# A two-block transformer kernel: the mixer's input products taken from x before its norm, the norm's row factor applied when the products leave PSUM, and retention's value products placed beside attention

## The chip, the core and the metric

One core of one Trainium2 chip runs the whole program. The metric is the device time of one execution in microseconds (us). The engines are PE (TensorE, matmuls into PSUM; its weight loads are listed as PEld), DVE (VectorE), ACT (ScalarE), POOL (GpSimd) and SP, whose queue issues all DMAs. Each engine works through its own list of instructions in order and waits on semaphores that the others raise.

## The reference, cut to what matters

Only the first steps of the first block are touched. x is 512 x 1024, float32, and everything is computed in float32.

```python
def rms_norm(x, g):
    y = x * lax.rsqrt(jnp.mean(x * x, axis=-1, keepdims=True) + RMS_EPS)
    return y * g

def hybrid_mixer(h, w_in, attn_gn_g, ret_gn_g, w_out):      # h = rms_norm(x, pre_mix_g)
    proj = h @ w_in                                        # 1024 -> 7 x 512
    aq, ak, av, rq, rk, rv, rg = jnp.split(proj, splits, axis=-1)
    a = dilated_attention(rope(aq), rope(ak), av)          # 8 heads of 64
    a = a * lax.rsqrt(jnp.mean(a * a, axis=-1, keepdims=True) + RMS_EPS)
    r = retention(rope(rq), rope(rk), rv)                  # 4 heads of 128
    r = silu(rg) * group_norm(r)
    return concat(a, r) @ w_out
```

Behind it come a cross-attention to a memory (`mem`, 256 rows, which has its own norm and value and key products), a SwiGLU, and a second block. They stay as they are.

## The kernel before

**Tiling.** x lies transposed in SBUF: 8 tiles of 128 features x 512 tokens (`XT`). A float32 product is made as three matmuls of rounded operands (`three`, L376): each operand is split into a high part (rounded to float32r) and a low part (the rest), and high x low, low x high and high x high are summed in PSUM. A 128 x 1024 chunk of weights (512 KB) is loaded into one of six slots, its high part is made by ACT (`hi_to`, L349; two buffers, so chunk i waits until chunk i-2 has been used), its low part by DVE (`lo_to`, L359). One chunk feeds 24 matmuls of 128x512 (three per k tile). Chunks are used in the order aq (0 to 3), ak (4 to 7), av (8 to 11), rq, rk, rg (12 to 23), rv (24 to 27), then the memory's values (28 to 35).

**Start of the mixer** (`mix_in_*`, L498 to L563). SP loads the 8 tiles of x, the tables `c0`, the gains (`small`), six weight chunks and the table `c1`. ACT squares the tiles of x, PE sums them over the features with a matrix of ones (`sums_pe`, 8 float32 matmuls, two buffers for the squares, so ACT and PE take turns), ACT makes the root (`root_act`: Ln and Exp), DVE multiplies each tile by gain and row factor (`scaled_dve`), ACT rounds the high part (`high_act`) and DVE takes the low part. Only then can the first product start. Then come the 8 tiles of q and k (`QK`), one weight chunk each: 24 matmuls, ACT's eviction from PSUM to SBUF, one float32 matmul with a permutation (`permA`) that turns the just evicted tile for the rotary embedding, and DVE's three operations of `rotate_dve`. PE waits in every tile for the eviction. Last come the 96 matmuls of av.

**Rest and attention** (`mix_rest_*`, `attend_*`). Python generators are interleaved by `weave` (L189): in each slot one step of the products of rq, rk and rg, one step of attention, and one more step of products. Attention has 32 units (4 query blocks x 8 heads) in 40 slots (`attend_slots`, L646): in slot n the scores of unit n, the transposition of unit n-2 and the value product of unit n-3; after the last unit of a query block its output is divided, squared on POOL, normed, multiplied on POOL (`a_gn`) and transposed by PE. The products of the rest are used up after 22 slots.

**Retention and memory** (`mid_*`). The order of each engine is written out as a string of letters (`TURNS0`, L795; `walk_streams`): r is the products of rv (PE) or their evictions (ACT), m the memory's norm, s retention's scores (DVE: the decay that takes them out of PSUM), i its outputs, w the rounding of the next weight chunk, V the memory's value products, M on ACT a Silu of a small vector, t a transposition. PE's scores and the row sum take four PSUM banks in turn (`low`). The memory's norm begins with 15 operations of 128x256 on POOL (`mem_pool`), which start when `mem` has been loaded; SP issues that load only when all events of the list `mixed` have come.

## Time and profile before

| | us |
|---|---|
| median of 3 runs | 2443.28 (2442.37 to 2444.06) |
| the profiled execution | 2444.46 |
| its span in the trace | 2442.6 |
| PE busy / DVE / ACT / POOL | 2338.0 / 1291.4 / 961.9 / 343.1 |
| mean granted PE clock | 0.985 |

The stages that the change touches lie in the first 306 us of the span: the start of the mixer until 114.6, rest and attention until about 249, the products of rv until about 274, retention until 294, then the memory's values. The profiled execution took 1.2 us more than the median. A granted clock of 1.00 is 2.4 GHz and 0.50 is 1.2 GHz. A float32 matmul shows as two records, a matmul of rounded operands as one.

### The profile page before, as it was taken

How to read it: one execution, taken by the hardware profiler on the slowest of the kernel's cores; microseconds unless marked ns; L12 is line 12 of the kernel's file. 1: busy time of each engine (PE TensorE's matmuls, PEld its weight loads, DVE VectorE, ACT ScalarE, POOL GpSimd, SP SyncE). 2: the span in 40 equal slices, each digit the busy share in tenths (PEclk: the TensorE clock that was granted, in tenths of full speed). 3: DMA queues.
4: the chain of work that ended last, by engine and by line, in shares of the span. 5: the costliest groups of instructions: out<-in, count | busy, mean ns of one | idle time of the engine just before them, and what ended most of it. 6: DMA issues, size and time to landing. Idle time of an engine off the chain costs nothing.

```text
span 2442.6 us, 29369 instructions
## 1 busy us (share of the span) xinstructions
PE 2338.0 (96%) x11798; PEld 1880.8 (77%) x11798; DVE 1291.4 (53%) x1982; ACT 961.9 (39%) x1672; POOL 343.1 (14%) x338
## 2 busy tenths in 40 slices
PE   6999998989999997999999999999999999899999
PEld 3677787768878884899998898776666788688887
DVE  3344547457757426766666777424464533542442
ACT  3235344443222225544534545345544422431331
POOL 0000214131101110232222333100111001000000
PEclk9999998999999998999999999999999999899999
DMA  4220222225565222110000011110101334232332
GB/s 159 78 67 29 83 99 96 86 104 172 185 212 188 62 74 80 61 57 27 27 27 18 18 35 53 35 53 20 41 20 53 104 109 135 70 97 95 95 98 83
DMA packets 60037, 195.69 MB, mean 80 GB/s; under 512 B 6656, under 2 KB 11520, under 8 KB 59520
## 3 DMA queue, kind: packets, MB, share of 16 engines
q1 hardware_dynamic: 59904, 193.83, 24.1%
q8 instruction: 94, 1.54, 0.3%
q14 instruction: 39, 0.32, 0.0%
HBM read 187.25 MB, written 6.55 MB: 79 GB/s over the span
## 4 chain that ended last, share of the span: by engine, by line
PE 89%; DVE 7%; ACT 2%; issue 1%; POOL 1%; DMA 0%; SPq 0%; DVEq 0%; ACTq 0%
PE ps L132 84%; PE ps L135 4%; DVE sb L165 2%; DVE sb L157 2%; DVE r L157 1%; ACT sb L144 1%; ACT r L144 1%; DVE r L165 1%; POOL sb L157 0%; ACT L142 0%; DVE sb L162 0%; DMA sb<-in_w_aq 0%; POOL sb L148 0%; SPq L186 0%; POOL sb L162 0%
## 5 line engine op out<-in xcount | busy, mean ns | idle before, releaser
L132 PE MATMUL ps<-r 128*128 128x512 f32 (+1 forms) x7032 | 1606.1, 387 | 46.4 <-DVE r L157 20.3
L132 PEld LDWEIGHTS ps<-r 128*128 128x128 f32 x7032 | 1282.7, 190 | 328.2 <-issue 48.1
L132 PE MATMUL ps<-sb 128*128 128x128 f32 (+5 forms) x3768 | 694.8, 332 | 49.4 <-ACT sb L144 32.0
L157 DVE TENSOR_TENSOR r<-sb,r 128x1024 fp32r<-128x1024 f32 (+3 forms) x413 | 431.1, 1054 | 446.4 <-ACT r L144 445.4
L132 PEld LDWEIGHTS ps<-sb 128*128 128x128 f32 x3768 | 505.2, 191 | 196.3 <-issue 110.1
L144 ACT ACTIVATE r<-sb 128x1024 fp32r<-128x1024 f32 (+3 forms) x437 | 377.9, 884 | 601.3 <-PE ps L132 452.1
L157 POOL TENSOR_TENSOR sb<-sb 128x512 f32<-128x512 f32 (+3 forms) x222 | 265.6, 1203 | 1552.4 <-ACT sb L144 990.8
L144 ACT ACTIVATE sb<-ps 128x512 f32<-128x512 f32 (+2 forms) x526 | 232.5, 462 | 515.8 <-PE ps L132 340.7
L157 DVE TENSOR_TENSOR sb<-ps,sb 128x512 f32<-128x512 f32 (+3 forms) x274 | 162.2, 602 | 214.0 <-PE ps L132 207.1
L165 DVE SCALAR_TENSOR_TENSOR sb<-sb 128x512 f32<-128x512 f32 (+5 forms) x232 | 242.8, 1057 | 38.4 <-ACT sb L144 36.3
L144 ACT ACTIVATE sb<-sb 128x512 f32<-128x512 f32 (+6 forms) x300 | 153.8, 528 | 75.2 <-POOL sb L157 26.2
L157 DVE TENSOR_TENSOR sb<-sb 128x512 f32<-128x512 f32 (+2 forms) x158 | 129.4, 819 | 92.7 <-ACT sb L144 88.2
L135 PE MATMUL ps<-sb 128*128 128x128 f32 (+1 forms) x998 | 144.4, 275 | 5.6 <-POOL sb L157 4.6
L165 DVE SCALAR_TENSOR_TENSOR sb<-ps,sb 128x128 f32<-128x128 f32 (+1 forms) x232 | 86.7, 412 | 117.7 <-PE ps L132 111.7
L135 PEld LDWEIGHTS ps<-sb 128*128 128x128 f32 (+1 forms) x998 | 115.2, 142 | 33.7 <-issue 12.0
L144 ACT ACTIVATE sb<-ps,sb 128x128 f32<-128x128 f32 (+3 forms) x181 | 82.2, 465 | 126.6 <-PE ps L132 126.0
L142 ACT ACT_TABLE_LOAD x67 | 86.0, 1283 | 71.5 <-PE ps L132 46.0
L162 DVE TENSOR_SCALAR sb<-sb 128x1 f32<-128x1 f32 (+6 forms) x136 | 65.1, 484 | 49.2 <-ACT sb L144 46.2
L157 DVE TENSOR_TENSOR sb<-sb,ps 128x512 f32<-128x512 f32 (+2 forms) x128 | 60.7, 484 | 46.5 <-PE ps L132 45.7
L162 POOL TENSOR_SCALAR sb<-sb 128x128 f32<-128x128 f32 x80 | 56.7, 715 | 175.4 <-PE ps L132 125.3
L148 DVE COPY sb<-ps 128x512 f32<-128x512 f32 (+5 forms) x76 | 38.4, 512 | 38.8 <-PE ps L135 31.8
L145 ACT ACTIVATE sb<-ps,sb 128x768 f32<-128x768 f32 (+1 forms) x48 | 39.1, 819 | 25.3 <-DVE sb L162 19.5
(24 smaller groups left out, 189.3 us busy)
## 6 DMA issues: line engine op xcount, KB each, us to landing
sb<-in_w_mlp SPq DMA_DIRECT2D x64, 512.0 KB, 3.5
sb<-in_w_mod SPq DMA_DIRECT2D x48, 512.0 KB, 4.6
sb<-in_w_qkv SPq DMA_DIRECT2D x24, 512.0 KB, 3.7
sb<-in_w_g SPq DMA_DIRECT2D x20, 512.0 KB, 3.9
sb<-in_w_u SPq DMA_DIRECT2D x20, 512.0 KB, 4.0
sb<-in_w_out SPq DMA_DIRECT2D x16, 512.0 KB, 3.6
sb<-in_w_down SPq DMA_DIRECT2D x16, 512.0 KB, 3.7
sb<-in_w_gate SPq DMA_DIRECT2D x16, 512.0 KB, 3.7
```

The source lines that it names most:

```text
L132: return QUIET if self.e is None else self.e.matmul(o, l, r, start=start, stop=stop)
L135: return QUIET if self.e is None else self.e.transpose(o, i, ident)
L142: self.e.preload_act_table_set(self.set)
L144: return self.e.activation(o, i, f, bias=bias, scale=scale)
L145: return self.e.activation(o, i, f, bias=bias, scale=scale, accum_out=acc)
L148: return QUIET if self.e is None else self.e.tensor_copy(o, i)
L157: return QUIET if self.e is None else self.e.tensor_tensor(o, a, b, op)
L162: return self.e.tensor_scalar(o, a, s1, None, op0) if op1 is None else self.e.tensor_scalar(o, a, s1, s2, op0, op1)
L165: return QUIET if self.e is None else self.e.scalar_tensor_tensor(o, a, s, b, op0, op1)
```

## The change

1. **Start.** The gains are loaded first, then two tiles of x and one weight chunk in turn. ACT rounds x times gain (without the row factor) as each tile arrives, DVE takes the low part from it. The products of aq start from that: `w_aq` is now stored by rows, and `project_four` makes all four tiles of q at once in four banks, chunk by chunk. Squares are made by ACT beside it and added up on POOL (`add_squares`); PE sums them in two matmuls (`row_sum_pe`) after aq. The row factor lies in `RX` (along tokens) and, by four transpositions, in `RCOL` (one per partition).
2. **Row factor at eviction.** q, k, rq, rk are evicted by DVE with a multiplication by `RX`, rg too, before ACT's Silu; av and rv by ACT with the scale `RCOL`. ACT evicts no q, k, rq or rk tile any more.
3. **Turnings later.** The matmul with `permA` runs at least one tile after its product (`swap`); three of them lie between the chunks of av. The table `c1` is loaded in two parts.
4. **rv beside attention.** After 16 empty steps the 96 matmuls of rv follow in `mix_rest_pe`, in slots 30 to 37 of attention; their weight chunks are rounded there. The order strings lose PE's r and move w, s and m; SP waits for the last score (`a_s`, 31) instead of `mixed` before it loads `mem`. ACT and DVE wait for `mixed` in their own lists.

```diff
-C1 = {"maskA": 512, "cosA": 512, "sinA": 512, "cosR": 512, "sinR": 512, "decay": 2048, "permA": 128, "permR": 128}
+C1 = {"permA": 128, "cosA": 512, "sinA": 512, "maskA": 512, "cosR": 512, "sinR": 512, "decay": 2048, "permR": 128}
...
-        columns("w_aq", range(4))
+        rows("w_aq", 0)
...
+        RX, RCOL = T0 + 6656, T0 + 7232
...
         def mix_in_sp(e, got):
-            for k in range(KT):
-                e.dma(S(XT + k * NT, NT), D["xT"][:, k * NT:(k + 1) * NT]).then_inc(*land(f"x{k}", "in"))
+            e.dma(S(SM, NSMALL), D["small"]).then_inc(*land("small_in"))
+            for i in range(4):
+                for k in (2 * i, 2 * i + 1):
+                    e.dma(S(XT + k * NT, NT), D["xT"][:, k * NT:(k + 1) * NT]).then_inc(*land(f"x{k}", "in"))
+                load_to(e, got, i)
             e.dma(S(CO["ident"], sum(C0.values())), D["c0"]).then_inc(*land("c0_in"))
-            e.dma(S(SM, NSMALL), D["small"]).then_inc(*land("small_in"))
-            load_to(e, got, 5)
-            e.dma(S(W, sum(C1.values())), D["c1"]).then_inc(*land("c1_in"))
...
         def mix_in_pe(e):
-            sums_pe(e, "mix", 0)
-            for i, (name, base, mt) in enumerate(QK):
...
+            whole(project_four(e, CI["w_aq", 0], HT, HL, "mix_lo", bs))
...
+            whole(row_sum_pe(e, "mix", take))
+            key(0)
...
+            for i in range(4):
+                t = e.transpose(P(b * 512 + i * 128, 128), S(RX + i * 128, 128), IDN)
...
+            key(1)
+            swap(0)
+            key(2)
+            swap(1)
+            swap(4)
+            key(3)
+            swap(2)
+            swap(5)
+            bs = [take() for _ in range(4)]
+            values = project_rows(e, CI["w_av", 0], toks_of(HT, HL, NT, 4, "mix_lo"), bs)
+            for i in (3, 6, 7):
+                swap(i)
+                for _ in range(4):
+                    next(values)
+            whole(values)
...
         def mix_in_act(e, got):
-            hi_to(e, got, 1)
-            squares_act(e, "mix", lambda k: S(XT + k * NT, NT), lambda k: [(f"x{k}", "in")])
-            root_act(e, "mix", R0)
-            high_act(e, "mix", HL)
...
+            for k in range(KT):
+                e.wait_ge(*at(f"x{k}", "in"))
+                e.act(R(HT + k * NT, NT), S(XT + k * NT, NT), ACT.Copy, scale=sm("pre_mix_g", k)).then_inc(*up("mix_hi", k))
+                if k % 2:
+                    hi_to(e, got, k // 2)
+                    square_act(e, "mix", k - 1, S(XT + (k - 1) * NT, NT))
+                    square_act(e, "mix", k, S(XT + k * NT, NT))
+            hi_to(e, got, 5)
+            root_act(e, "mix", RX, sums=("mix_zsum", 1))
...
-                e.act(S(aV + b * 512, 512), P(b * 512, 512), ACT.Copy).then_inc(*up("av_ev", b))
+                e.act(S(aV + i * 512, 512), P(BK["av", i] * 512, 512), ACT.Copy, scale=S(RCOL + i, 1)).then_inc(*up("av_ev", i))
...
+            def out_of(i):
+                name, base, mt = QK[i]
+                e.wait_ge(*at("mix_rs"))
+                e.wait_ge(*at("w_used", CI["w_aq", 0][-1] if i < 4 else CI[name, mt][0]))
+                e.stt(S(base + mt * NT, NT), P(BK["qk", i] * 512, NT), 0.125 if i < 4 else 1.0, S(RX, NT), MU,
+                      MU).then_inc(*up("qk_ev", i))
...
+            for _ in range(16):
+                yield
+            yield from project_rows(e, CI["w_rv", 0], toks_of(HT, HL, NT, 4, "mix_lo"), range(4))
...
-                        e.act(S(base + mt * NT, NT), P(BK["rk", i] * 512, NT), ACT.Copy).then_inc(*up("rk_ev", i))
...
+                        e.tt(S(base + mt * NT, NT), P(BK["rk", i] * 512, NT), S(RX, NT), MU).then_inc(*up("rk_ev", i))
...
-                e.act(S(rgT + mt * NT, NT), P(BK["rg", mt] * 512, NT), ACT.Silu).then_inc(*up("rg_ev", mt))
...
+                e.act(S(rgT + mt * NT, NT), S(rgT + mt * NT, NT), ACT.Silu).then_inc(*up("rg_ev", mt))
...
+                e.tt(S(rgT + mt * NT, NT), P(BK["rg", mt] * 512, NT), S(RX, NT), MU).then_inc(*up("rg_x", mt))
...
-            "PE": ("rrrrrrrrrrrrrrrrrmmssssssssissssisssssiiiVVVVtVVVVtVVVVttVVVVVtoooooooooooooooooKKeKKqqqqqqqeqKKxxxx"
+            "PE": ("ssssssssmmissssisssssiiiVVVVtVVVVtVVVVttVVVVVtoooooooooooooooooKKeKKqqqqqqqeqKKxxxx"
...
         def mem_act(e):
+            fence(e, mixed)
...
         def mid_sp(e, got):
-            for x in mixed:
-                e.wait_ge(*at(*x))
+            e.wait_ge(*at("a_s", 31))
             e.dma(S(memT, 2048), D["memT"]).then_inc(*land("mem_in"))
...
         def gpsimd(e):
+            whole(add_squares(e, "mix"))
             attend_pool(e)
...
-        A["w_" + n] = wN(part) if n in ("av", "rv") else wT(part)
+        A["w_" + n] = wN(part) if n in ("aq", "av", "rv") else wT(part)
```

In the following rows of the program's order, r is a rounded operand, ps is PSUM, sb other SBUF; the names in brackets are semaphores (norm_lo: low part of an x tile; w_lo, w_hi: low and high part of a weight chunk; evicted, by_row: a tile taken out of PSUM by ACT, or with the row factor by DVE; rot_t: PSUM bank of a turning read; a_exp, a_pt0, a_pt1: attention; r_s, r_d: retention's scores made, taken out).

PE at the start of the program, before:

```order
L132 MATMUL ps<-sb 128x512 [waits c0_in,squares]
L132 MATMUL ps<-sb 128x512 [waits squares] x7
L132 MATMUL ps<-r 128x512 [waits norm_lo,w_lo]
...
L132 MATMUL ps<-sb 128x512 [waits table_in,evicted]
L132 MATMUL ps<-r 128x512 [waits w_lo]
L132 MATMUL ps<-r 128x512 x23
L132 MATMUL ps<-sb 128x512 [waits root_ln,evicted]
```

and after:

```order
L133 MATMUL ps<-r 128x512 [waits norm_lo,w_lo]
L133 MATMUL ps<-r 128x512 x11
L133 MATMUL ps<-r 128x512 [waits norm_lo]
...
L133 MATMUL ps<-sb 128x512 [waits pool_add,c0_in]
L133 MATMUL ps<-sb 128x512 [waits end_zsq]
L133 MATMUL ps<-r 128x512 [waits w_lo]
L133 MATMUL ps<-r 128x512 x23
L136 MATMUL ps<-sb 128x128 [waits root_rs]
...
L133 MATMUL ps<-sb 128x512 [waits c1_rot,by_row]
L133 MATMUL ps<-r 128x512 [waits by_row,w_lo]
```

The 8 sums have gone from the front; two of them stand behind the 96 matmuls of aq, and the turning stands a tile of k later.

ACT from the last norm of attention to the memory's norm, before:

```order
L144 ACTIVATE sb<-sb 128x8 [waits root_ln]
L142 ACT_TABLE_LOAD
L144 ACTIVATE sb<-sb 128x16
L144 ACTIVATE r<-sb 128x1024 [waits w1]
L144 ACTIVATE r<-sb 128x1024 [waits w_used,w2]
L144 ACTIVATE r<-sb 128x1024 [waits w_used,w3]
L144 ACTIVATE r<-sb 128x1024 [waits w_used,w4]
L144 ACTIVATE sb<-ps 128x512 [waits w_used]
L144 ACTIVATE sb<-ps 128x512 x3
L142 ACT_TABLE_LOAD [waits sums]
```

and after:

```order
L145 ACTIVATE r<-sb 128x1024 [waits w_used,w3]
L145 ACTIVATE sb<-sb 128x8 [waits a_red]
L145 ACTIVATE sb<-sb 128x8 [waits root_ln]
L145 ACTIVATE sb<-ps,sb 128x512 [waits w_used]
L145 ACTIVATE sb<-ps,sb 128x512 x3
L143 ACT_TABLE_LOAD
L145 ACTIVATE sb<-sb 128x16
L145 ACTIVATE r<-sb 128x1024 [waits w4]
L143 ACT_TABLE_LOAD [waits root_rs,evicted,a_gn,rot_rot,sums,a_y,turned]
```

The rounding of the chunk in slot w4 (chunk 28, the memory's first) stood ahead of rv's four evictions; it now stands behind them, behind a table load and the Silu of the 16-column vector.

DVE at the same place, before:

```order
L174 TENSOR_REDUCE sb<-sb 128x8 [waits pool_sq]
L157 TENSOR_TENSOR sb<-ps,sb 128x4x128 [waits turned]
L157 TENSOR_TENSOR r<-sb,r 128x1024 [waits w_hi] x4
L157 TENSOR_TENSOR sb<-ps,sb 128x512 [waits r_s]
L157 TENSOR_TENSOR sb<-ps,sb 128x384 [waits r_s]
```

and after (the second row is the low part of chunk 28, the last but two that of chunk 29):

```order
L158 TENSOR_TENSOR sb<-ps,sb 128x4x128 [waits turned]
L158 TENSOR_TENSOR r<-sb,r 128x1024 [waits root_rs,a_gn,evicted,w_hi,rot_rot,a_y]
L158 TENSOR_TENSOR sb<-ps,sb 128x512 [waits r_s]
...
L158 TENSOR_TENSOR sb<-ps,sb 128x256 [waits r_s]
L158 TENSOR_TENSOR r<-sb,r 128x1024 [waits w_hi]
L158 TENSOR_TENSOR sb<-ps,sb 128x128 [waits r_s]
L166 SCALAR_TENSOR_TENSOR sb<-sb 128x256 [waits root_rs]
```

Retention's decays stand behind the low part of chunk 28 in both; the eighth now stands behind that of chunk 29 as well, whose high part ACT makes after the memory's root.

## Rows read from the trace of the kernel before

**Rows 1.** The page's part 4: the chain that ended last, by engine.

```profile
PE 89%; DVE 7%; ACT 2%; issue 1%; POOL 1%; DMA 0%; SPq 0%; DVEq 0%; ACTq 0%
```

**Rows 2.** Timeline of PE: start, us, operation, count, [idle before, releaser].

```profile
15.19 9.38 PE L132 MATMUL ps<-sb 128*128 128x512 f32 x16 [15.19 <-ACT sb L144]
29.56 7.22 PE L132 MATMUL ps<-r 128*128 128x512 f32 x18 [4.99 <-DVE r L157]
...
39.49 1.13 PE L132 MATMUL ps<-sb 128*128 128x512 f32 x2 [0.69 <-ACT sb L144]
...
92.57 22.01 PE L132 MATMUL ps<-r 128*128 128x512 f32 x96 [0.88 <-DVE sb L157]
...
115.36 2.32 PE L132 MATMUL ps<-r 128*128 128x512 f32 x9 [0.78 <-ACT sb L144]
```

**Rows 3.** PE timeline, then windows: length; busy PE, PEld, DVE, ACT, POOL; clock; DMA; GB/s.

```profile
15.19 2.07 PE L132 MATMUL ps<-sb 128*128 128x512 f32 x2 [15.19 <-ACT sb L144]
...
16.00:18.00 2.00, 2.00 (x4) 0.67 (x2) 0.00 (x0) 0.63 (x1) 0.00 (x0) 1.00 1.21 497
```

**Rows 4.** SP's queue (timeline), then the first DMA issue: KB, us to landing.

```profile
0.72 3.70 SPq L186 DMA_DIRECT2D sb<-in_xT  x8
...
sb<-in_xT SPq DMA_DIRECT2D x1, 256.0 KB, 3.2
```

**Rows 5.** Timelines of ACT and DVE at the start: rounding one weight chunk.

```profile
12.27 1.06 ACT L144 ACTIVATE r<-sb 128x1024 fp32r<-128x1024 f32 x1 [10.27 <-DMA sb<-in_w_aq]
13.56 1.06 ACT L144 ACTIVATE r<-sb 128x1024 fp32r<-128x1024 f32 x1 [0.23 <-DMA sb<-in_w_aq]
...
13.36 2.51 DVE L157 TENSOR_TENSOR r<-sb,r 128x1024 fp32r<-128x1024 f32 x2 [12.48 <-ACT r L144]
```

**Rows 6.** Timeline of PE around the change from attention to retention.

```profile
249.18 1.12 PE L135 MATMUL ps<-sb 128*128 128x128 f32 x4 [4.39 <-POOL sb L157]
249.95 23.97 PE L132 MATMUL ps<-r 128*128 128x512 f32 x96
274.70 2.66 PE L132 MATMUL ps<-sb 128*128 128x256 f32 x8 [0.78 <-ACT sb L144]
277.86 16.58 PE L132 MATMUL ps<-sb 128*128 128x128 f32 x106 [0.50 <-DVE sb L157]
294.19 5.73 PE L132 MATMUL ps<-r 128*128 128x512 f32 x24
```

**Rows 7.** Timeline of POOL: one 128x512 sum or product.

```profile
229.16 1.04 POOL L157 TENSOR_TENSOR sb<-sb 128x512 f32<-128x512 f32 x1 [16.10 <-DVE sb L157]
```

**Rows 8.** Timeline of ACT in the same stretch.

```profile
248.03 1.28 ACT L142 ACT_TABLE_LOAD   x1
...
249.44 1.04 ACT L144 ACTIVATE r<-sb 128x1024 fp32r<-128x1024 f32 x1
...
273.96 2.06 ACT L144 ACTIVATE sb<-ps 128x512 f32<-128x512 f32 x4 [4.32 <-PE ps L132]
```

**Rows 9.** The attention stretch in windows, columns as in rows 3.

```profile
115.00:245.00 130.00, 129.18 (x620) 91.80 (x620) 58.49 (x130) 58.08 (x122) 6.26 (x6) 1.00 0.15 49
```

**Rows 10.** Timelines of DVE, then POOL, in the same stretch.

```profile
250.33 0.69 DVE L157 TENSOR_TENSOR sb<-ps,sb 128x512 f32<-128x512 f32 x1 [2.90 <-PE ps L135]
...
258.79 1.72 DVE L157 TENSOR_TENSOR r<-sb,r 128x1024 fp32r<-128x1024 f32 x1 [6.63 <-ACT r L144]
...
255.92 12.78 POOL L157 TENSOR_TENSOR sb<-sb 128x256 f32<-128x256 f32 x15 [6.79 <-DMA sb<-in_memT]
```

**Rows 11.** PE behind two short pauses (timeline), and the clock there (windows).

```profile
391.54 8.74 PE L132 MATMUL ps<-r 128*128 128x512 f32 x25 [2.94 <-DVE r L165]
...
396.00:398.00 2.00, 2.00 (x7) 1.62 (x6) 2.00 (x2) 0.00 (x0) 2.00 (x1) 0.63 0.00 0
...
547.65 7.29 PE L132 MATMUL ps<-r 128*128 128x512 f32 x24 [2.91 <-DVE r L165]
...
550.00:552.00 2.00, 2.00 (x8) 1.62 (x7) 2.00 (x3) 1.25 (x2) 0.00 (x0) 0.73 0.00 0
```

## What the change does to the time, predicted

> **What bounds the kernel now.** I read the chain of work that ended last first: PE holds 89% of it [rows 1], so the question everywhere is which wait PE meets, and whether the work there is PE's own. Then the timeline of PE through the stages that the diff touches. It shows a front of 29.56 us in which PE does only the eight sums, at 15.19 to 24.57, and pauses another 4.99 us before the first product [rows 2]. After that each tile of q and k costs 24 matmuls, a turning of 1.12 us and a wait of 0.69 us for ACT's eviction, and av's 96 matmuls take 22.01 us, which is 0.229 us each or 5.5 us per chunk [rows 2]. They end at 114.58.
>
> The clock needs two views. The granted clock says 1.00 at the first sum, yet that sum, the same two records as a turning, took 2.07 us where the turning took 1.12 [rows 2, 3]. So durations say that PE began at 1.2 GHz, whatever the column says. The Trainium skill (TensorE: Matmul & The Clock Gate, What's actually happening) says that the throttled clock is the default and that activity releases it; this trace's durations agree. By the column the first products of the new kernel would lose nothing, by the page and the durations about 2 us.
>
> **Start, new.** PE's first product needs `small`, two tiles of x and the first weight chunk: 140 + 512 + 512 = 1164 KB. Before, the first 256 KB landed at 0.7 + 3.2 = 3.9 us [rows 4] and the first weight chunk, the 2956th KB, at 12.25 (ACT waited for it until 12.27) [rows 5]: 323 KB per us. So chunk 0 lands at 3.9 + 908/323 = 6.7; ACT's high part 1.06, DVE's low part 1.25 [rows 5], semaphores 0.2: first product at 9.2 us. Bounds: 8.5 if the rate is that between the first two chunks (512 KB in 1.3 us [rows 5]), 10.2 if ACT's two copies of x and DVE's low parts come in the way.
>
> From there PE's own work: aq 22.0, two sums 2.2, ak 22.0, four transpositions 0.6 (1.12 at half clock [rows 6]), eight turnings 9.0, av 22.0, together 77.8. Half clock at the start: sums one and two lost about 1.9 us before; pauses elsewhere were followed by 3.4 to 5.9 us at half clock (below), half of it lost. I take 2.0, bounds 0 and 3.0.
>
> Do the others keep up? Per chunk of aq (5.5 us on PE) ACT has two copies of x, two squares (each under 0.7, since 1024 columns take 1.06 [rows 5]), a chunk's high part and a wait for POOL's sum of 1.04 [rows 7]: at most 4.9 us. DVE has under 3 us, POOL 2.1. Transfers are 1 MB per chunk, 3.1 us. The high part of chunk i waits for chunk i-2 to be used, which is the case a whole chunk ahead. So it is covered, with 0.6 us to spare on ACT; that cover is thin. The root (table load 1.28 [rows 8] and two operations) and four evictions hide beside the first tile of k. The evictions are DVE's now; every turning has a tile of 5.5 us between its product and itself, so the eight waits of 0.69 are gone, and behind each turning DVE's rotation (2.1 us) and a low part (1.25) again fit into 5.5. I allow 0.5 us for small waits (0 to 2.5). av ends at 9.2 + 77.8 + 2.0 + 0.5 = 89.5, against 114.58: 25.1 saved. The first bank that the rest takes holds the second evicted tile of av, so the wait of 0.78 [rows 2] becomes 1.3. Net **24.6**; the rest starts at 90.8.
>
> **Attention and rest.** PE is busy 129.18 of 130 us there [rows 9]: its own work. The twelve evictions (0.69 each on DVE, by the size of a decay [rows 10], against 0.6 on ACT) lie on an engine busy 58 of 130 us, and PE touches the bank again only after a turning and an attention unit. Cost 0; -0.5 to +4 as bounds, because DVE's queue now also holds attention's maxima behind the wait for each tile.
>
> rv's 96 matmuls are the same work in another place. What goes is what lay around them: 4.39 us of pause while DVE, POOL and ACT norm the last block, and the half clock behind it, 23.97 - 22.01 = 1.96 us [rows 2, 6]. In the new order 42 matmuls (9.6 us) stand between attention's last value product and the last transpositions, which more than cover the 4.4 us chain. Saved **6.35**. Without that pause rv would end at 90.8 + (273.92 - 115.36) - 6.35 - 0.6 (transpositions, now behind it) = 242.4; call this E.
>
> **Retention: a new wait.** Before, ACT rounded chunks 25 to 28 while rv ran. Now the high part of chunk 28 stands behind rv's evictions, a table load and a Silu, and DVE's low part of chunk 28 stands ahead of every decay. So from E: evictions 2.06, load until the high part begins 1.41, high part 1.04 [rows 8], low part 1.25 alone or 1.72 beside POOL's squares, first decay 0.69 [rows 10]: E + 6.55 to E + 7.05. PE meanwhile: transpositions, 0.15 for the first eviction, the four scores of head 0 (1280 columns at 1.12 per 512: 2.8), until E + 3.55. The fifth score needs the bank of the first decay: PE pauses **3.25 us** (3.0 to 3.9). POOL's 12.78 us of squares [rows 10] start some 5 us before E and are done by E + 8, when PE gets to the memory's sum at E + 9.6 at the earliest, so they don't add to it; without the early load of `mem` they would.
>
> The Trainium skill (SBUF — State Buffer, SBUF: two separate sides) has DVE and POOL take a shared pair of ports in turn, the loser blocked for a whole operation. The row of 1.72 against 1.25 agrees in sign. By that rule a whole POOL operation (0.85) may stand before the low part: E + 7.4 and 2418.4 in all, where the row gives E + 7.05 at most.
>
> Does that pause cost clock? The two shortest long pauses of the trace, 2.94 and 2.91 us, were both followed by half clock, until 397.48 (0.63 over the window from 396 to 398 is half clock for 1.48 us of it; 5.9 us after PE's start) and 551.1 (3.4) [rows 11]. So yes: half of the mean of 4.7 is lost, **2.35** (0 to 3.0). Then a second wait: the eighth decay stands behind the low part of chunk 29, behind ACT's high part, behind the memory's root. From the memory's sum: table load 1.28, Ln and Exp 0.9, high part 1.05, low part 1.23, decay 0.3, 4.8 us; PE has an output head (1.8) and two scores (2.0) to do: it waits **1.0**.
>
> Before, E to the first value product of the memory (294.19) took 20.27 us with 1.28 of waits [rows 6]: 18.99 of work. Now 0.6 + 18.99 + 0.15 + 3.25 + 2.35 + 1.0 = 26.3. The 0.6 of transpositions only changed sides, so **5.4** is lost. That product starts at 268.7, and everything behind it keeps its form: DVE ends its memory norm then as before, about when retention's last output comes.
>
> **Sum.** 24.6 + 6.35 - 5.4 = 25.5, the same as 294.19 - 268.7: 2444.46 - 25.5 = 2419.0 for the profiled execution, and, as that stood 1.2 above the median, **2417.8**. All good ends together (0.7 + 2.0 + 0.5 + 0.5 + 0.25 + 2.35) give 2411.5, all bad ones (1.0 + 1.0 + 2.0 + 4.0 + 0.65 + 0.65) 2427.
>
> **Rivals.**
> *No pause in retention.* If the waits of 3.25 and 1.0 and the half clock don't come, because decays aren't held up by chunk 28, 6.6 us return: 2411. Against it: the order rows, DVE keeps its order. 0.10.
> *The start is fed too slowly.* ACT's and POOL's 4.9 us per chunk are near PE's 5.5; if squares and sums take 1.5 us each more, or the mixed small and large transfers run slower, PE pauses per chunk and stays at half clock. Price: four chunks at 1.5 and 3 us more of half clock's loss, 9 us partly inside my bounds: 2424. For it: POOL's rows vary. 0.12.
> *rv fills nothing.* Its chunk roundings stand in DVE's and ACT's lists between attention's operations; if each of four delays PE by 1.5 us, the 6.35 are gone: 2424. 0.07.
> *DVE becomes the bound in attention.* Twelve tiles each hold a wait for PE, an eviction, a rotation and a low part in front of attention's maxima. At 2.0 us per tile the gain is gone (12 x 2.0 = 24): 2441, 0.03. From 2.2 us per tile on the kernel is slower; with all that can stand in the way (0.69 + 1.41 + 1.25 = 3.35 us) it is 2418 + 40 = 2458: 0.03. Against both: attention's scores stand two units ahead of their transpositions, and DVE is busy 45%.
>
> **How the numbers follow.** My forecast has 0.65, the rivals 0.10, 0.12, 0.07, 0.03, 0.03. The range 2411 to 2427 takes in the first four nearly whole and leaves out the last two and the ends. Under 5 us (0.2%) a measurement can't tell a change: faster 0.94, same 0.03, slower 0.03.
>
> **What the new profile would show.** First product on PE near 9.2 us and at about twice 0.229 us each for the first few; no pause over 0.5 us until av ends near 89.5; the memory's first value product near 268.7, a PE pause of about 3 us some 4 us after rv's last matmul, released by DVE, with granted clock 0.50 behind it; no pause of 4.39 us before the last transpositions. I am wrong if a row of pauses released by ACT or DVE stands in the first 33 us, if attention with rv takes over 155 us, or if stages behind 300 us have changed by more than 2.

## The result

The changed kernel takes 2414.82 us (median of 4 runs, 2413.76 to 2415.65), the kernel before 2442.87 beside it (4 runs, 2442.37 to 2444.06): a ratio of 0.9884 with a 95% interval of 0.9867 to 0.9901, 28.05 us less. The prediction was 2417.8, its range 2411 to 2427. The profiled execution took 2415.65 us, its span is 2413.8.

The first two lines are parts 1 and 4 of its page (busy time and share; the chain that ended last by engine), to be set against [rows 1]. PE holds 96% of the span, as before, and is busy 12 us less with the same products. Six of the eight sums are gone (9.38 us of records before [rows 2], 1.88 for the two that are left); the rest I didn't split. The mean granted clock, 0.988 against 0.985, says nothing about the change: executions of the kernel before alone lie between 0.985 and 0.988.

```profile
PE 2326.1 (96%) x11790; PEld 1877.0 (78%) x11790; DVE 1300.0 (54%) x1995; ACT 953.2 (39%) x1656; POOL 352.4 (15%) x344
...
PE 89%; DVE 7%; ACT 2%; issue 1%; POOL 1%; DMA 0%; SPq 0%; DVEq 0%; ACTq 0%
```

The timeline of PE through the start (start, us, operation, count, [idle before, releaser]) answers to [rows 2]:

```profile
10.89 23.46 PE L133 MATMUL ps<-r 128*128 128x512 f32 x96 [10.89 <-DVE r L158]
34.19 1.88 PE L133 MATMUL ps<-sb 128*128 128x512 f32 x4
...
47.33 1.02 PE L133 MATMUL ps<-sb 128*128 128x512 f32 x2
...
53.67 1.88 PE L133 MATMUL ps<-sb 128*128 128x512 f32 x4
...
88.64 2.33 PE L133 MATMUL ps<-r 128*128 128x512 f32 x9 [1.45 <-ACT sb L145]
90.89 0.48 PE L133 MATMUL ps<-sb 64*128 64x128 f32 x2
```

There is one wait between 10.89 and 90.89: the 1.45 us for av's evictions. A turning (two records) shows as 1.02 or 1.13 us long [rows 2], but the start of the next group tells what it costs PE: from 47.33 to 53.67, a turning and a tile of products, 6.34 us pass, and the tile's 24 matmuls are 5.5 of them. So a turning occupies PE for 0.85 us, where nothing is waited for. Before the change such a tile took 7.28 us (39.49 to 46.77, the turning, 24 matmuls and a wait of 0.69), so a wait that shows as 0.69 cost 0.94: a group behind a wait costs PE about 0.25 us more than its gap shows.

The timeline of PE from the end of attention to the memory's first value product, against [rows 6]:

```profile
239.69 0.60 PE L136 MATMUL ps<-sb 128*128 128x128 f32 x4
240.72 2.40 PE L133 MATMUL ps<-sb 128*128 128x512 f32 x8 [0.43 <-ACT sb L145]
246.89 9.84 PE L133 MATMUL ps<-sb 128*128 128x512 f32 x34 [3.77 <-DVE sb L158]
257.13 10.12 PE L133 MATMUL ps<-sb 128*128 128x256 f32 x72 [0.40 <-DVE sb L158]
267.01 5.70 PE L133 MATMUL ps<-r 128*128 128x512 f32 x24
```

The pause of 4.39 us ahead of the last transpositions is gone, and one of 3.77 stands behind the scores of head 0. The timelines of ACT and DVE there name its cause, against [rows 8, 10]: ACT's four evictions, table load, Silu, then the high part of chunk 28 at 243.75, for which DVE waits 3.90 us; DVE's first decay follows its low part at 246.06.

```profile
239.89 2.42 ACT L145 ACTIVATE sb<-ps,sb 128x512 f32<-128x512 f32 x4 [5.54 <-PE ps L133]
242.33 1.28 ACT L143 ACT_TABLE_LOAD   x1
...
243.75 1.04 ACT L145 ACTIVATE r<-sb 128x1024 fp32r<-128x1024 f32 x1
...
244.92 1.22 DVE L158 TENSOR_TENSOR r<-sb,r 128x1024 fp32r<-128x1024 f32 x1 [3.90 <-ACT r L145]
246.06 1.68 DVE L158 TENSOR_TENSOR sb<-ps,sb 128x512 f32<-128x512 f32 x4
```

Windows of 2 us there (length; busy PE, PEld, DVE, ACT, POOL; granted clock; DMA) show half clock from about 246 until 252.8, of which PE works 5.95 us:

```profile
246.00:248.00 2.00, 1.11 (x2) 0.62 (x3) 1.74 (x5) 0.00 (x0) 1.34 (x2) 0.51 0.00 0
...
252.00:254.00 2.00, 2.00 (x15) 1.91 (x15) 0.00 (x0) 1.53 (x2) 0.00 (x0) 0.79 0.00 0
```

Where the time went, by landmarks of PE in the two profiled executions:

| | before | after | saved by then |
|---|---|---|---|
| first product | 29.56 | 10.89 | |
| start of the rest | 115.36 | 88.64 | 26.7 |
| last transpositions of attention | 249.18 | 239.69 | (rv is behind them before, ahead of them after) |
| memory's first value product | 294.19 | 267.01 | 27.2 |
| end of the span | 2442.6 | 2413.8 | 28.8 |

Nearly all of the gain is made in the first 89 us. The move of rv saved 0.5 us more in these two, and the last 1.6 us lie in the part that the change doesn't touch.

### The profile page after: what moved, and what is told of

Its sections match the earlier page's. It is cut to its first block, busy times and chain, and to the rows that moved or that the text cites. A ratio compares the mean times of both kernels' runs of the same rounds, so it can differ in the third digit from the quotient of the medians.

```text
span 2413.8 us, 29380 instructions
## 1 busy us (share of the span) xinstructions
PE 2326.1 (96%) x11790; PEld 1877.0 (78%) x11790; DVE 1300.0 (54%) x1995; ACT 953.2 (39%) x1656; POOL 352.4 (15%) x344
## 4 chain that ended last, share of the span: by engine, by line
PE 89%; DVE 7%; ACT 2%; issue 1%; POOL 1%; DMA 0%; SPq 0%; DVEq 0%; ACTq 0%
PE ps L133 85%; PE ps L136 4%; DVE sb L166 2%; DVE sb L158 2%; DVE r L158 2%; ACT sb L145 1%; ACT r L145 1%; DVE r L166 1%; ACT L143 0%; POOL sb L158 0%; DVE sb L163 0%; POOL sb L149 0%; DMA sb<-in_w_aq 0%; POOL sb L163 0%; SPq L187 0%
## 5 line engine op out<-in xcount | busy, mean ns | idle before, releaser
L133 PEld LDWEIGHTS ps<-sb 128*128 128x128 f32 (+1 forms) x3756 | 506.6, 192 | 173.4 <-issue 115.9
L158 POOL TENSOR_TENSOR sb<-sb 128x512 f32<-128x512 f32 (+3 forms) x228 | 275.1, 1213 | 1513.6 <-ACT sb L145 1000.5
L145 ACT ACTIVATE sb<-ps 128x512 f32<-128x512 f32 (+3 forms) x498 | 216.2, 454 | 457.5 <-PE ps L133 278.5
L158 DVE TENSOR_TENSOR sb<-ps,sb 128x512 f32<-128x512 f32 (+3 forms) x286 | 170.3, 605 | 204.5 <-PE ps L133 194.2
L145 ACT ACTIVATE sb<-sb 128x512 f32<-128x512 f32 (+5 forms) x304 | 156.4, 529 | 80.0 <-POOL sb L158 33.1
L136 PE MATMUL ps<-sb 128*128 128x128 f32 x1002 | 144.5, 275 | 1.2 <-DVE sb L149 0.6
L145 ACT ACTIVATE sb<-ps,sb 128x128 f32<-128x128 f32 (+2 forms) x189 | 86.8, 474 | 136.7 <-PE ps L133 136.1
L136 PEld LDWEIGHTS ps<-sb 128*128 128x128 f32 x1002 | 115.5, 141 | 29.7 <-issue 12.7
L149 DVE COPY sb<-ps 128x512 f32<-128x512 f32 (+6 forms) x77 | 38.5, 507 | 40.5 <-PE ps L136 33.5
```

The lines of the kernel that those rows point to most:

```text
L133: return QUIET if self.e is None else self.e.matmul(o, l, r, start=start, stop=stop)
L136: return QUIET if self.e is None else self.e.transpose(o, i, ident)
L145: return self.e.activation(o, i, f, bias=bias, scale=scale)
L149: return QUIET if self.e is None else self.e.tensor_copy(o, i)
L158: return QUIET if self.e is None else self.e.tensor_tensor(o, a, b, op)
```

## Experiments

All were timed beside the kernel before on the same chip. The medians of the kernel before were 2443.49 (e1, e2, e7, e3), 2442.90 (e8, e4, e5, e9) and 2442.67 (e0, e10, e4b, e6). The executions of one kernel lie 0.4 to 4.6 us apart, so for effects of 1 to 3 us I read landmarks of the trace, and the medians only beside them.

**rv back behind attention (e1_rv_behind).** The front and the early load of the memory stay.

```diff
-            for _ in range(16):
-                yield
-            yield from project_rows(e, CI["w_rv", 0], ...)      # in mix_rest_pe
+        def rv_pe(e, low): ...                                  # as in the kernel before, order strings too
```

> The changed kernel with retention's values (rv, 96 matmuls) put back behind attention, as in the kernel before; the new front and the early load of the memory stay. My theory: beside attention rv saves 6.35 us (a pause of 4.39 and 1.96 of half clock), and chunk 28's late rounding gives nearly all of it back in retention (pause 3.77, half clock 3.0). So undoing it changes almost nothing: the rest starts at 88.6 as now, and from there the kernel before took 294.19 - 115.36 = 178.8 us to the memory's first value product, so that it starts at 267.5 (now 267.0) and the time is 2415 (2412 to 2418). Rival: retention's pause does not come from the move and would be there anyway; then rv behind attention costs its full 6.35, the product starts at 273.4 and the time is 2421.

2416.99 us (2416.58 to 2417.23). PE's timeline has the old pause and the slow rv products again:

```profile
222.59 1.12 PE L136 MATMUL ps<-sb 128*128 128x128 f32 x4 [4.39 <-POOL sb L158]
223.36 23.66 PE L133 MATMUL ps<-r 128*128 128x512 f32 x96
...
267.65 4.60 PE L133 MATMUL ps<-r 128*128 128x512 f32 x19
```

(The last line is cut short by the window; the product has 24 matmuls.) The memory's first value product starts at 267.65, with the rest starting where it did (88.62). The changed kernel has it at 267.01, with the rest at 88.64, and, run once more, at 266.29, with the rest at 88.87. My theory gave 267.5, the rival 273.4. Counted from the start of the rest, the move saved 0.7 and 1.6 us: it takes out a pause of 4.39 us with its half clock and puts in one of 3.77 with its own.

**Chunk 28 rounded ahead of rv's evictions (e2_chunk28_early).** The high part goes to the end of `mix_rest_act`, the low part to the end of `mix_rest_dve`; the order strings lose their first w, and chunk 29's high part stands behind the evictions.

```diff
                 hi_to(e, got, c)
                 for _ in range(4):
                     yield
+            hi_to(e, got, CI["w_rv", 0][-1] + 1)
...
-            "ACT": ("rrrrrMMwmwmmm...      "DVE": ("wssssssswsmmm...
+            "ACT": ("rrrrrwMMmmm...        "DVE": ("sssswssssmmm...
```

> The changed kernel with both roundings of chunk 28 (the first of the memory's values) put ahead of rv's evictions, and chunk 29's high part right behind them. My theory: the pause of 3.77 us behind head 0's scores and its half clock (3.0) go. What is late next is POOL's squares of the memory, which end at 247.4, some 1.9 us after PE has done the scores of two heads (245.5). The memory's first value product then starts at 262 (261.5 to 263) instead of 267.0, and the time is 2409.8. Rival: the pause is not chunk 28's; it moves to another wait within head 0 and head 1, the product starts at 266 or later and the time stays at 2414 or above. A second one: the two roundings hold up attention's last maxima or exponentials, so that the last transpositions start later than 239.7.

2413.08 us (2411.05 to 2415.46), the product at 265.94. In its timelines of PE and POOL the 3.77 is gone and the scores of two heads stand in one row, but a wait of 3.12 for POOL follows, and the clock is at half again:

```profile
241.26 4.55 PE L133 MATMUL ps<-sb 128*128 128x512 f32 x16 [0.43 <-ACT sb L145]
248.94 17.25 PE L133 MATMUL ps<-sb 128*128 128x256 f32 x98 [3.12 <-POOL sb L158]
...
234.97 13.91 POOL L158 TENSOR_TENSOR sb<-sb 128x512 f32<-128x512 f32 x16 [1.37 <-ACT sb L145]
...
248.00:250.00 2.00, 1.06 (x3) 0.89 (x4) 0.00 (x0) 0.00 (x0) 0.80 (x2) 0.50 0.00 0
```

So chunk 28 was the cause of the pause of 3.77, and the rival was half right: a pause came at another wait. I had put the next one at 1.9 us and without half clock. POOL's row (the last multiplication of attention and the memory's 15 operations) took 13.91 us instead of 12.99, because a second low part of DVE now lies beside it (see the section on the prediction). Attention ended 0.5 later because of the start, and the pause of 3.12 us was followed by half clock as the one of 3.77 was.

**POOL's squares early as well (e8_squares_early).** Four of the memory's eight squares go into POOL's idle time.

```diff
         def attend_pool(e):
+            squares_of_mem = mem_pool(e)
             for qb in range(4):
+                if qb == 3:
+                    for _ in range(4):
+                        next(squares_of_mem)
                 e.wait_ge(*at("a_div", qb))
...
+            whole(squares_of_mem)
```

> As the kernel with chunk 28 rounded ahead of rv's evictions, and POOL makes the first four of the memory's eight squares (and their sums) ahead of attention's last two operations instead of behind them; the memory lands at 221.7 us, POOL is idle from 208.5 to 231. My theory: in that kernel PE waited 3.12 us for POOL in front of the memory's sum, with 5.4 us of half clock behind it (2.7 lost). Both go: POOL ends at about 242, PE gets to the sum at 245.8, no granted clock under 1.00 between 240 and 256, the memory's first value product starts at 260 (259 to 261) where it stood at 265.94, and the time is 2407.3. Rival: the norm of the memory (DVE's and ACT's eight tiles each) then ends last, and the values wait for it: product at 262 to 264 behind a wait for DVE or ACT, time 2410.

2408.81 us (2406.75 to 2410.73). PE's timeline, a window, and POOL's timeline:

```profile
245.98 14.60 PE L133 MATMUL ps<-sb 128*128 128x256 f32 x98 [0.24 <-DVE sb L158]
260.33 5.71 PE L133 MATMUL ps<-r 128*128 128x512 f32 x24
...
250.00:252.00 2.00, 2.00 (x15) 1.00 0.00 0
...
222.38 5.99 POOL L158 TENSOR_TENSOR sb<-sb 128x256 f32<-128x256 f32 x7 [13.43 <-DMA sb<-in_memT]
```

The product starts at 260.33, 260 expected, with 0.43 and 0.24 us of waits ahead of it and the clock at 1.00. From the last transpositions to this product it is 20.18 us, against 27.32 in the changed kernel: these two late helpers and the clock behind them cost 7.1 us (6.2 against the changed kernel's second run, which took 26.38). The rival, that the norm of the memory would end last, fell: behind the scores no wait over 0.24 stands ahead of the values.

**The start: transfers held back (e7_hold), x ahead of all chunks (e3_x_first).**

```diff
             for i in range(4):
+                if i == 1:
+                    e.wait_ge(*at("x0", "in"))                  # e7_hold
                 for k in (2 * i, 2 * i + 1):
                     e.dma(S(XT + k * NT, NT), ...)
-                load_to(e, got, i)                              # e3_x_first: behind the loop instead
```

> The changed kernel with SyncE waiting, after small, x0, x1 and chunk 0, until x0 has landed (4.7 us) before it issues x2 and what follows. My theory: chunk 0 landed at 8.5 us, not at the 6.7 that I had predicted, because the transfers issued behind it share the engines with it: 1.8 MB had moved by then, where small, two tiles of x and chunk 0 are 1.16 MB. Held back, they leave it the whole rate: chunk 0 lands at 7.0 (6.5 to 7.5), the first product starts at 9.4 instead of 10.89, and the time is 1.5 us less, 2413.3. Rival: the start-up rate itself is low, chunk 0 still lands at 8.5, the first product starts where it does now and the held transfers open pauses on PE in the first 33 us: time 2415 to 2418.

> The changed kernel with all eight tiles of x loaded ahead of the first weight chunk, as in the kernel before, where chunk 0 landed at about 12.25 us. This undoes only the mixing of the two in SyncE's queue. My theory: the first product starts at 14.5 us (14 to 15.5), 3.6 later than now, nothing behind it changes, and the time is 2418.4. Rival: with all of x there the products run without the half clock of the start or with ACT and DVE further ahead, and part of the delay comes back: under 2416.5.

ACT's timelines of the changed kernel, of e7_hold and of e3_x_first (the high part of chunk 0 is the first 128x1024):

```profile
4.71 1.28 ACT L145 ACT_TABLE_LOAD   x1 [4.71 <-DMA sb<-in_xT]
6.01 1.33 ACT L145 ACTIVATE r<-sb 128x512 fp32r<-128x512 f32 x2
8.52 1.06 ACT L145 ACTIVATE r<-sb 128x1024 fp32r<-128x1024 f32 x1 [1.18 <-DMA sb<-in_w_aq]
```

```profile
6.11 2.28 ACT L145 ACTIVATE r<-sb 128x512 fp32r<-128x512 f32 x3
```

```profile
11.60 1.06 ACT L145 ACTIVATE r<-sb 128x1024 fp32r<-128x1024 f32 x1 [4.35 <-DMA sb<-in_w_aq]
```

Held back, chunk 0 was there when ACT came to it (at 7.35 us, inside the group of three, one of which is its high part); the first product started at 9.71 and the memory's value product at 265.95. The time, 2415.22 (2413.93 to 2415.4), shows no gain. In nine runs in which the start was that of the changed kernel (its own two among them) the first product came at 9.80 to 10.89, 10.39 on the average, because chunk 0 was waited for until some moment between 7.4 and 8.5 us. So the one profiled run with the hold is 0.7 us ahead of their average, and 0.1 ahead of the best of them: less than the time can tell. I had expected 1.5 from the one run with the latest landing. That the transfers behind chunk 0 share the engines with it is in line with this and not proven by it. With x first, chunk 0 was waited for until 11.60, the first product came at 13.97 and the rest started at 92.37, 3.1 to 3.8 and 3.5 to 3.7 us later than in the two runs of the changed kernel. The memory's value product, at 269.76, was 2.8 to 3.5 later, and the time was 2418.15 (2416.23 to 2419.54). Up to the rest nothing of the delay came back, so the theory held; the shorter difference at the memory's product is retention's half clock, which varies from run to run (below).

**PE warm before the first product (e9_warm).**

```diff
             bs = [take() for _ in range(4)]
+            e.wait_ge(*at("small_in"))
+            for _ in range(9):
+                e.matmul(P(7 * 512, 256), S(SM, 128), S(SM, 256), True, True)
             whole(project_four(e, CI["w_aq", 0], HT, HL, "mix_lo", bs))
```

> The changed kernel with nine matmuls of 128x256 on the small table in front of the first product, into a bank that is not yet in use: PE is busy from about 3 us on with work that nobody reads. My theory: aq's 96 matmuls took 23.3 to 24.6 us in the runs so far instead of 22.0, because PE starts at half clock, whatever the column of the granted clock says; now they take 22.1 (22.0 to 22.6), aq ends 1.3 to 2.5 us earlier, and the time is 2413.2 (2412 to 2414). Rival: the slow first matmuls have another cause (transfers into SBUF that run beside them until 21 us, or the new weights), and they stay slow: 23.3 or more, time as before.

PE's timeline:

```profile
2.94 6.86 PE L133 MATMUL ps<-sb 128*128 128x256 f32 x18 [2.94 <-DMA sb<-in_small]
10.74 22.07 PE L133 MATMUL ps<-r 128*128 128x512 f32 x96 [0.94 <-DVE r L158]
```

22.07 us for the 96 matmuls, beside the same transfers; 23.4 to 24.6 in the nine other runs with this start. So the slow matmuls go with a PE that had done nothing before, not with the transfers, and cost 1.4 to 2.6 us here. (The first product itself didn't come earlier: 10.74.) The landmarks kept it: from the first product to the memory's first value product 254.7 us (10.74 to 265.47), against 256.1 in both runs of the changed kernel. The time, 2415.17 (2414.96 to 2415.4), didn't show it.

**Turnings at once (e4_turn_at_once, e4b_k_first).** Each of k's turnings directly behind its product, with the turning of a q tile between the two (e4) or behind them (e4b). The calls are written in one line here; DVE's order follows them, and the turnings 6 and 7 move out of av.

```diff
-            key(1); swap(0); key(2); swap(1); swap(4); key(3); swap(2); swap(5)
+            swap(4); key(1); swap(0); swap(5); key(2); swap(1); swap(6); key(3); swap(2); swap(7)    # e4
+            swap(4); key(1); swap(5); swap(0); key(2); swap(6); swap(1); key(3); swap(7); swap(2)    # e4b
```

> The changed kernel with each of k's four turnings directly behind its own product instead of a tile or more later (DVE's order follows). Undoes only the delay of k's turnings. My theory: PE waits for DVE's eviction in front of each of the four, 0.7 to 0.9 us, as it did before the change (0.69), and for nothing else: av's 96 matmuls end 3.0 us later than in the changed kernel (2.8 to 3.6; against the end of aq, which takes out the start), and the time is 2417.9. Rival: waiting there lets DVE get ahead, and av's first chunks or evictions come earlier, so that less than 1.5 us is lost.

> As the kernel with k's turnings directly behind their products, but with each ahead of the q turning that stood in front of it there, so that nothing lies between the product and its turning. That kernel lost nothing (one wait of 0.85 us, the other three hidden behind a turning of q of 0.85 us; from aq's end to the rest 54.3 us, and 54.45 in the changed kernel). My theory: now all four waits of 0.85 show, 2.5 us more, 56.9 from aq's end to the start of the rest, and the time is 2416.5. Rival: the waits are taken back at av, whose evictions the rest waits for or whose chunks come earlier: 54.3 to 55 again, 2414.

PE's timelines of e4, then of e4b (`x4` is two turnings):

```profile
43.67 1.12 PE L133 MATMUL ps<-sb 128*128 128x512 f32 x2 [0.85 <-DVE sb L166]
...
50.12 2.07 PE L133 MATMUL ps<-sb 128*128 128x512 f32 x4
```

```profile
42.91 1.13 PE L133 MATMUL ps<-sb 128*128 128x512 f32 x2 [0.85 <-DVE sb L166]
...
50.28 1.98 PE L133 MATMUL ps<-sb 128*128 128x512 f32 x4 [0.79 <-DVE sb L166]
```

e4 took 2413.09 us (2412.33 to 2416.34) where I expected 2417.9: I was wrong. One wait of 0.85 shows; in front of the other three PE has a turning of q to do, 0.85 us, and that covers the eviction but for 0.19 (two turnings and a tile take 7.40 us, 50.12 to 57.52, against 7.21 in the changed kernel). From the first sum behind aq to attention's first scores it is 56.60 us in e4, 56.70 in the changed kernel (34.19 to 90.89), 59.11 in e4b (34.24 to 93.35), 2.4 to 2.5 more with waits of 0.85, 0.79, 0.79 and 0.78. In both the wait of 1.45 for av's evictions has gone: by the kernel's own count of banks av's tiles lie in banks 1 to 4 here, and the rest takes bank 0 first, which holds av's second tile in the changed kernel. With 0.25 us added to each wait that shows, the sums come out within 0.1: e4 loses 1.1 and 0.6 (three times 0.19) and gains 1.7, e4b loses 4.2 and gains 1.7. That the 1.45 us could be had in the changed order too was not tried. e4b's time was 2414.49 (2414.09 to 2416.23), 2 us under what I expected, though its landmarks are where I expected them (below).

**DVE beside attention (e5_dve_twice, e6_act_evicts).** Two more operations ahead of each eviction of rq and rk on DVE, or these evictions on ACT as before the change (this variant leaves out the row factor of rq and rk).

```diff
+                        for j in range(2):                      # e5
+                            e.tt(...).then_inc(*up("twice", i, j)); e.wait_ge(*at("twice", i, j))
                         e.tt(S(base + mt * NT, NT), P(BK["rk", i] * 512, NT), S(RX, NT), MU).then_inc(*up("rk_ev", i))
...
+                        e.act(S(base + mt * NT, NT), P(BK["rk", i] * 512, NT), ACT.Copy).then_inc(*up("rk_ev", i))   # e6, for e.tt
```

> The changed kernel with two more operations of the eviction's size (128x512, 0.69 us each) on DVE in front of each of the eight evictions of rq and rk, each waited for, beside attention: 11.0 us of DVE's time in all. My theory: DVE is not what the stage waits for; the last transpositions of attention start within 0.3 us of where they stood (151.05 us behind the start of the rest), and the time stays at 2415 (2413.5 to 2416.5). Rival, that the evictions on DVE are near being the bound there: 1.4 us per tile come through, up to 11 us, 2426.

> The changed kernel with the eight evictions of rq and rk back on ACT as plain copies, as before the change; the row factor of these two is left out, so the scores of retention are computed from rows that are not normed. My theory: DVE's evictions cost nothing beside attention, since PE never waits there: from the start of the rest to attention's last transpositions 151.05 us as now (150.7 to 151.4), time 2414.8. Rival: twice 5.5 us more on DVE cost 3.1 there (154.1), so by the same rate the 5.5 that are there now cost 1.5, and without them it is 149.5 and the time 2413.3.

e6: 2415.66 us (2413.32 to 2416.17); from the start of the rest to attention's last transpositions 88.52 to 239.56, 151.04 us, as in the changed kernel (151.05). DVE's evictions of rq and rk cost nothing there. e5: 2417.38 (2415.34 to 2419.94), 88.07 to 242.19, 154.12 us: 3.1 of the 11 us came through, where the tiles of rq and rk lie. PE, without a gap there in the changed kernel, has 1.9 us of gaps between 100 and 160 us and none from 160 to 220; the rest of the 3.1 may be what a wait costs beyond its gap, which isn't shown. One window of the changed kernel, then of e5:

```profile
100.00:120.00 20.00, 20.00 (x89) 14.15 (x88) 11.52 (x26) 4.70 (x14) 0.00 (x0) 1.00 0.20 66
```

```profile
100.00:120.00 20.00, 18.75 (x81) 13.00 (x79) 12.68 (x27) 4.66 (x14) 0.00 (x0) 1.00 0.16 52
```

So both theories of e5 were wrong in size: the cover is real, but thin. The rate of 3.1 in 11 does not reach down to the evictions that are there now: as e6 shows, these are covered whole. e5's time lies 2.6 us above the changed kernel's first median, with its four executions 4.6 us apart.

**The changed kernel again (e0_after), and all that helped (e10_all).** e10 is e8 with e7's hold, eight matmuls on the small table, and a first activation of one element:

```diff
         def mix_in_act(e, got):
+            e.wait_ge(*at("eps6"))
+            e.act(S(MISC + 16, 1), S(EPS6, 1), ACT.Copy)
```

> The changed kernel as it is, once more, beside the next three on the same chip: 2414.8 (2413.5 to 2416). It also shows how far the start varies by itself: chunk 0 was waited for until 7.4, 7.9 and 8.5 us in runs with the same start, and the first product started at 9.8, 10.3 and 10.9. I expect 9.8 to 10.9 here, and aq's 96 matmuls in 23.3 to 24.7.

> All that helped, together: chunk 28 rounded ahead of rv's evictions, POOL's first four squares ahead of attention's last operations, SyncE holding back all but the first four transfers until x0 has landed, eight matmuls on the small table ahead of the first product, and a one-element activation on ACT at the very start, so that its table load of 1.28 us no longer stands behind the first tile of x. My theory: each works by itself, since they act on different waits: first product near 9.1 (8.8 to 9.8), aq's matmuls in 22.1, aq's end at 31.3 where the kernel with the squares early had it at 34.7; the memory's first value product at 257.0 (256.3 to 258), time 2405.4 (2404 to 2407.5). Rival: the start's gains are taken back by pauses on PE during aq, because x and chunks now arrive barely in time: aq ends at 33 or later and the time is 2407.5 to 2409.

e0_after: 2413.80 us (2412.76 to 2415.06), first product 10.15, aq in 24.43. e10_all: **2402.89 us** (2402.51 to 2404.36), 10.9 less than the changed kernel on the same chip, 39.8 less than the kernel before, ratio 0.9839 (0.9824 to 0.9854). ACT's, then PE's timeline:

```profile
0.71 1.28 ACT L145 ACT_TABLE_LOAD   x1 [0.71 <-PEq L3308]
...
6.93 1.06 ACT L145 ACTIVATE r<-sb 128x1024 fp32r<-128x1024 f32 x1 [0.84 <-DMA sb<-in_w_aq]
...
9.30 22.05 PE L133 MATMUL ps<-r 128*128 128x512 f32 x96 [0.25 <-DVE r L158]
31.19 1.88 PE L133 MATMUL ps<-sb 128*128 128x512 f32 x4
...
256.86 5.73 PE L133 MATMUL ps<-r 128*128 128x512 f32 x24
```

First product 9.30, end of aq 31.19, the memory's product 256.86, where I expected 9.1, 31.3 and 257.0. The parts add up, as they should if each acts on a wait of its own. The time came out 2.5 us better than expected, and that lies behind these landmarks.

**Behind the memory's first value product** all fourteen profiled executions run the same instructions to the end of the span. In the profiled executions it took 2143.8 us (e4) to 2148.5 (e8), 2148.4 before, 2146.8 and 2146.9 in the two of the changed kernel, 2144.1 in e4b, 2145.5 in e10. PE's idle time there is 68.8 to 72.9 us and its busy time 2073.2 to 2077.7, so most of the spread is matmuls that last longer. The granted clock of the whole run was 0.989 in the three shortest (e4, e4b, e10), and 0.985 and 0.987 in the two longest. One reason shows in the rows: the same pause of about 3 us was followed by half clock in one execution and not in another. Here is one of 3.07 us in the changed kernel, then in e10, with a window behind each:

```profile
364.28 7.93 PE L133 MATMUL ps<-r 128*128 128x512 f32 x26 [3.07 <-DVE r L166]
366.00:368.00 2.00, 2.00 (x6) 1.60 (x5) 2.00 (x3) 1.24 (x2) 1.92 (x3) 0.50 0.00 0
```

```profile
354.12 3.01 PE L133 MATMUL ps<-r 128*128 128x512 f32 x12 [3.07 <-DVE r L166]
356.00:358.00 2.00, 1.24 (x6) 0.69 (x6) 2.00 (x3) 1.25 (x2) 1.92 (x3) 1.00 0.00 0
```

I didn't take the spread apart further. Of the 28.8 us of the span, the last 1.6 are within it and can't be put down to the change.

## Why the prediction was right, point by point

**First product: mis-sized.** 9.2 (8.5 to 10.2) against 10.89, and 9.80 to 10.79 in the other runs with this start. What failed is the landing of chunk 0: it was waited for until 7.4 to 8.5 us, not 6.7. I had let it land at the running rate in the order of issue, while ten more transfers had been issued behind it by 8.5 us. ACT's table load behind the first tile of x (4.71 to 6.0), which I had left out, cost nothing here, since ACT was through with both tiles at 7.34 and then waited 1.18 for the chunk; it is what comes next once the others are held back (7.35 without a wait in e7). With both taken away (e10) chunk 0 was rounded at 6.93. From its landing to the first product it was 2.4 us, as reckoned (2.5).

**Half clock at the start: right.** 2.0 predicted, 1.4 to 2.6 found over the runs, 1.4 in the profiled one, and nothing in e9 and e10. The column of the granted clock reads 1.00 through it. What shows it is the count of matmuls in windows of 2 us (PE's part of the windows of the changed kernel), five at first and ten from 14 us on:

```profile
11.00:13.00 2.00, 2.00 (x5) 1.00 1.04 413
14.00:16.00 2.00, 2.00 (x10) 1.00 1.04 406
```

The Trainium skill (TensorE: Matmul & The Clock Gate, What's actually happening) has the throttled clock as the default that activity lifts. e9 agrees: behind 6.86 us of throw-away matmuls aq's 96 took 22.07 us.

**PE's work until av's end: mis-sized.** 77.8 + 0.5 + 2.0 = 80.3 predicted, 76.3 measured (10.89 to 87.19, which is 88.64 less the wait of 1.45). The step that failed is the 1.12 us for a turning: that is the length of its record behind a wait, where PE, without one, is kept for 0.85. The 7.28 us of such a tile before were rightly added up from 0.69, 1.12 and 5.5, but wrongly divided: 0.94 of them went with the wait. With eight turnings and two sums this is 2.7 of the 4 us; the rest is mainly the shorter half clock (0.6) and small waits that didn't come (0.5). The misses of this term and the one before had opposite signs: the front saved 26.7 where I had 24.6.

**Cover at the start: right, but thinner than thought.** POOL's sums took 1.28 to 2.09 us beside DVE, not 1.04 [rows 7], and ACT waited about 2 us for them three times:

```profile
13.39 2.09 POOL L158 TENSOR_TENSOR sb<-sb 128x512 f32<-128x512 f32 x1 [1.41 <-ACT sb L145]
...
15.51 0.63 ACT L145 ACTIVATE sb<-sb 128x512 f32<-128x512 f32 x1 [2.20 <-POOL sb L158]
```

It stayed hidden because the squares are wanted only at 34.19. The eight waits for evictions are gone; that a turning needs no whole tile of cover, but about 1 us (0.85 left 0.19 in e4), was an oversight that the sum didn't notice.

**Attention and rest: right.** 151.6 us predicted from the start of the rest to the last transpositions, 151.05 measured, and within 0.05 of it in e0, e2, e3, e6, e7, e8, e9 and e10. DVE's evictions of rq and rk cost 0 (e6). The pause of 4.39 was covered by rv.

**Retention: the mechanism right, sizes off by up to 0.7.** The pause of 3.25 (3.0 to 3.9) was 3.77. With E, the end of rv, at 239.69 it ended at E + 7.20 instead of E + 6.8, mainly because rv's evictions with a scale from SBUF took 2.42 us instead of 2.06 [rows 8], and it began at E + 3.43 instead of E + 3.55, with 0.43 instead of 0.15 for the first wait and 2.40 instead of 2.8 for the four scores. Its half clock cost 3.0 against 2.35, at the edge of its bound. The second wait was 0.40 (0.71 in e0) against 1.0. Together 27.32 us from the last transpositions to the memory's value product, predicted 26.3. The nine runs with this form of retention fall into two groups, four at 27.3 (the changed kernel, e6, e7, e9) and five at 26.3 to 26.4 (e0, e3, e4, e4b, e5): the pause is 3.77 or 3.78 in all, but the 34 matmuls behind it last 9.6 to 9.9 us in the first group and 8.5 to 8.6 in the second, so what differs is how long the half clock lasts. The prediction said of POOL's squares that they don't add; true in the changed kernel, and only because chunk 28 was later still, as e2 showed.

The Trainium skill (SBUF — State Buffer, SBUF: two separate sides) gives the pair of ports that DVE (with two inputs from SBUF) and POOL share to the operation that starts first, for its whole length, and blocks the other. That was a rival for DVE's low part of chunk 28, at E + 7.4; here it took 1.22 us, the same as alone. The traces agree with the rule all the same. In the changed kernel this low part began at 244.92, just as one operation of POOL ended, and it is POOL that was blocked: its next operation, one of 0.61 to 0.74 us otherwise, took 1.62. In e2 the low part began inside an operation of POOL and took 1.53, and POOL's next one took 1.59. Single operations, of POOL in the changed kernel (count, busy us, mean ns) and of DVE in e2:

```profile
L158 POOL TENSOR_TENSOR sb<-sb 128x256 f32<-128x256 f32 x1 | 1.6, 1619 | 0.1
...
236.14 1.53 DVE L158 TENSOR_TENSOR r<-sb,r 128x1024 fp32r<-128x1024 f32 x1 [1.82 <-ACT r L145]
```

So each low part beside the squares costs POOL about 0.9 to 1.0 us, and DVE up to 0.5 (the 1.72 of [rows 10]), by where in POOL's operation it begins.

**Sum.** 24.6 + 6.35 - 5.4 = 25.5 predicted by the memory's first value product, 27.2 measured: the front gave 2.1 more, attention and rv 0.6 more, and retention cost 1.0 more. The profiled execution was 3.35 us under its forecast of 2419.0; the other 1.6 of these lie behind that product and have no cause in the change. That the total came so close is luck in part: the first product was 1.7 us late, and PE's work behind it 4.0 us shorter. The rivals fell: "no pause in retention" by the row of 3.77, "the start is fed too slowly" by a PE without a wait in aq, "rv fills nothing" and "DVE becomes the bound" by the 151.05 us. That a retention without the pause was to be had at all, e8 shows. What the front gave is read from landmarks: no run undoes it as a whole, e3 undoes the order of the loads (3.5 to 3.7 us by the start of the rest) and e4b the delay of k's turnings (2.4 us).

## What to carry to other kernels

Before moving work into a pause, list what the other engines did beside it in its old place: here the roundings of the next chunk and POOL's squares lost their cover, and took back all but 0.7 to 1.6 us of the 6.35 until they were moved too. When a wait is removed, the next one is found only by running it; e2 alone would have looked like a failure. In front of a wait for an eviction, other work of its length covers nearly all of it (a turning of another tile left 0.19 us), and small differences are to be read from landmarks in the trace, since the time of the whole hides 1 to 3 us.

## What was unexpected of the hardware

- The granted clock reads 1.00 from the start of the execution, while PE's first 7 to 13 matmuls (the first 3 to 6 us of its work) run at half rate: 5 in 2 us, not 10, and 23.4 to 24.6 us for aq's 96 instead of 22.07. Matmuls on data that nobody reads, ahead of them, remove this.
- Pauses of 3.12 and 3.77 us were both followed by half clock; those of 0.85 and 1.45 were not. The length alone doesn't decide it: the same pause of 3.07 us was followed by half clock in one run and not in another, and one of 3.30 us (until 1886.25 in the changed kernel) was not.
- DVE's low part of a chunk (128x1024) and POOL's operations stand in each other's way: one of POOL of 0.6 to 0.7 us took 1.62 beside a low part that had begun first, and a low part of 1.22 us took 1.53 and 1.72 where POOL's had.
- The moment until which chunk 0 is waited for varies by 1.1 us (7.4 to 8.5) between runs with the same start.
- The first activation's table load (1.28 us) waits for that activation's data: with a one-element activation ahead of it it ran at 0.71 instead of 4.71.
- Four evictions of 128x512 on ACT with a scale per partition read from SBUF took 2.42 us, with a constant scale 2.06 [rows 8].
